# Reordering five seams of a two-block language-model kernel: opening, output operand, first up pairs, start of the down product, gate end

## The reference

```python
# block 1
u = rmsnorm(h, norm_mix); proj = u @ w_in
h = h + concat([sliding_window_sink_attention(q, k, v), gated_deltanet(...)]) @ w_o
m = rmsnorm(h, norm_mlp); h = h + square(relu(m @ w_up)) @ w_down
gate = sigmoid(rmsnorm(h, norm_ple) @ w_ple_gate); h = h + gate * (p @ w_ple_proj)
x = rmsnorm(h, norm_final)
# block 2
u = rms_norm(x, norm_mix_g) @ w_in_2
x = x + concat([pool_mixer(u_pool), hgrn2_mixer(...)]) @ w_out_2
h2 = rms_norm(x, norm_mlp_g_2); x = x + square(relu(h2 @ w_up_2)) @ w_down_2
out = rms_norm(x, final_norm_g_2)
```

## Time and profile before

| | us |
|---|---|
| median of 3 runs | 2700.65 (2698.46 to 2703.38) |
| the profiled execution, its own time | 2696.92 |
| its span, first to last instruction | 2695.1 |
| PE busy in the span | 2551.9 (95%) |
| DVE / POOL / ACT busy | 1953.6 / 1077.8 / 956.4 |

### The profile page before, as it was taken

One profiled execution on the slowest core, in us unless ns is written; L12 is line 12 of the kernel. 1 busy time (PEld: TensorE's weight loads), 2 busy tenths in 40 slices (PEclk: granted clock), 3 DMA queues, 4 the chain that ended last, 5 costly groups with the idle time before them and its releaser, 6 DMA issues. The chain is left out here.

```text
span 2695.1 us, 34099 instructions
## 1 busy us (share of the span) xinstructions
PE 2551.9 (95%) x12634; PEld 2073.5 (77%) x12634; DVE 1953.6 (72%) x2511; ACT 956.4 (35%) x1452; POOL 1077.8 (40%) x675
## 2 busy tenths in 40 slices
PE   8889999989999998999998999999899999999997
PEld 5757887878678887887777788888786888778885
DVE  3677565564878789888948666767558787798887
ACT  3154232131633334444423133333316333344343
POOL 3412112142345555445444433333333555454443
PEclk9999999999999999999999999999999999999999
DMA  4200000021044346444111200000211443554342
GB/s 156 71 16 23 15 18 23 16 86 32 24 158 151 139 161 219 172 169 159 47 48 47 104 32 31 31 26 29 94 40 63 146 159 137 208 195 140 126 156 94
DMA packets 109375, 253.53 MB, mean 94 GB/s; under 512 B 9280, under 2 KB 9536, under 8 KB 107072
## 3 DMA queue, kind: packets, MB, share of 16 engines
q1 hardware_dynamic: 104112, 234.15, 24.9%
q10 hardware_dynamic: 5136, 17.70, 2.0%
HBM read 182.08 MB, written 67.11 MB: 92 GB/s over the span
## 5 line engine op out<-in xcount | busy, mean ns | idle before, releaser
L607 PE MATMUL pairs<-x_hi,w_hi 128*128 128x512 f32 x1592 | 554.2, 412 | 55.8 <-DVE x_lo L1476 15.3
L607 PE MATMUL pairs<-x_lo,w_hi 128*128 128x512 f32 x1592 | 530.6, 397 | 0.0
L607 PE MATMUL pairs<-x_hi,w_lo 128*128 128x512 f32 x1592 | 528.9, 396 | 0.0
L571 POOL TENSOR_TENSOR idle<-idle 128x1 f32<-128x1 f32 x78 | 26.7, 342 | 936.8 <-PE pairs L607 924.0
L607 PEld LDWEIGHTS pairs<-x_hi,w_hi 128*128 128x128 f32 x1592 | 289.3, 192 | 139.6 <-issue 66.8
L607 PEld LDWEIGHTS pairs<-x_hi,w_lo 128*128 128x128 f32 x1592 | 301.1, 191 | 63.9
L607 PEld LDWEIGHTS pairs<-x_lo,w_hi 128*128 128x128 f32 x1592 | 301.3, 191 | 63.4
L607 PE MATMUL mid<-work_r,w_hi 128*128 128x512 f32 x992 | 315.2, 400 | 26.0 <-POOL w_lo L590 12.3
L607 PE MATMUL pairs<-work_r,w_hi 128*128 128x512 f32 x1072 | 329.9, 391 | 4.1 <-DVE work_r L1476 1.8
L590 POOL TENSOR_TENSOR w_lo<-w_raw,w_hi 128x512 fp32r<-128x512 f32 x150 | 237.3, 1589 | 236.5 <-ACT w_hi L1074 236.4
L590 POOL TENSOR_TENSOR w_lo<-work,w_hi 128x512 fp32r<-128x512 f32 x128 | 178.5, 1396 | 221.5 <-ACT w_hi L1074 221.4
(11 more groups left out here) (192 smaller groups left out, 4250.6 us busy)
## 6 DMA issues: line engine op xcount, KB each, us to landing
h_ops<-work SPq DMA_DIRECT2D x224, 256.0 KB, 4.3
w_raw<-w_stream SPq DMA_DIRECT2D x81, 512.0 KB, 3.5
w_raw<-w_up SPq DMA_DIRECT2D x120, 256.0 KB, 3.9
out_sq<-h_ops SPq DMA_DIRECT2D x28, 1024.0 KB, 5.0
x_lo_raw<-h_ops SPq DMA_DIRECT2D x28, 1024.0 KB, 5.0
work<-w_down SPq DMA_DIRECT2D x16, 1024.0 KB, 7.1
out_sq<-w_down SPq DMA_DIRECT2D x8, 1024.0 KB, 7.2
x_lo_raw<-w_down SPq DMA_DIRECT2D x8, 1024.0 KB, 5.4
```

Of the source, the lines that this page charges most:

```text
L571: nc.gpsimd.tensor_tensor(idle[:, 0:1], idle[:, 1:2], idle[:, 1:2], ALU.add)
L607: return nc.tensor.matmul(out, w, x, start=start, stop=stop)
```

## The change

1. **Opening.** Unit 1 is loaded ahead of tile 2, the constants behind tile 6. ACT makes `x_hi` and the square of a tile one after the other. PE runs unit 1 four parts behind unit 0, in alternation; the sums of squares come in two groups of four, after the last part of unit 0 with its partner and after the next part of unit 1; `log_rows` comes before the last part of unit 1. `unit_started` of unit 1 is raised at its fifth part.
2. **`proj_with_norm`** (first unit of each MLP): squares in two groups of four, after the parts of tiles 1 and 3 (before: six groups after the parts of tiles 0 to 5), `log_rows` after the part of tile 5 (before: after all).
3. **Output operand.** The last but one head of both mixers is taken out of the hardware loops of ACT and DVE (`then_last`). In it `mix` tiles 0 to 5 are split: in the delta rule tiles 0 and 1 around the head's norm on ACT and DVE and 2 to 5 after it, in HGRN2 all six after it, and before the head's last `take`. The last head splits tile 6 alone.
4. **First up pairs.** `up_sum(1, 3)` moves from the first up step to right after `up_sum(1, 2)`, ahead of the plain pair's results (`first_y`).
5. **Start of down.** SP loads A11 of the first chunk between two groups of stores of pair 14, and the second operand (`load_h(1)`) after A12. The half slots of the first eight down steps are taken in the order in which the up steps leave them (`slot_index`, `slot_user`), so ACT prepares steps 105 to 110 four ahead (before: 106 and 107 from step 104 on); it makes none at 107 and 110 and two at 108 and 111.
6. **Gate end.** `x_hi` and `x_lo` of tiles 1 to 7 go in one row ahead of the last two tiles' squares and adds.

```diff
+        def slot_index(g):
+            if g < U_STEPS:
+                return (1, 0, 2, 3)[g % 4]
+            turn, k = divmod(g - U_STEPS, 4)
+            return ((0, 2, 3, 1), (0, 2, 1, 3), (0, 1, 2, 3))[min(turn, 2)][k]
+        def slot_user(g):
+            return max(k for k in range(g) if slot_index(k) == slot_index(g))
...
             for j in range(KT):
                 sp.dma_start(res[:, j, :], x_t[:, j, :]).then_inc(x_in[j], 16)
                 if j == 1:
+                    sp.dma_start(w_raw[:, 1, :], w_stream[1]).then_inc(w_loaded[1], 16)
+                if j == 6:
                     sp.dma_start(cst[:, :], consts).then_inc(consts_in, 16)
-                if j == 3:
-                    sp.dma_start(w_raw[:, 1, :], w_stream[1]).then_inc(w_loaded[1], 16)
...
                         load_h(0)
-                        load_h(1)
-                        store_rest(i - 1)
-                    store_last(i - 1)
...
+                        store_rest(i - 1, (2, 7))
                         sp.wait_ge(s["step_done"], g + 3)
                         load_down(0, A11)
+                        store_rest(i - 1, (5, 6))
+                        store_last(i - 1)
                         load_down(0, A12)
+                        load_h(1)
...
-                    for j in ((0, 1), (2,), (3,), (4,), (5,), (6, 7), (), ())[kt]:
-                        square_sum(n, j, squares[j])
-                log_rows(n)
+                    if kt in (1, 3):
+                        for j in range(2 * kt - 2, 2 * kt + 2):
+                            square_sum(n, j, squares[j])
+                    elif kt == KT - 3:
+                        log_rows(n)
...
-            att_unit(0)
-            pe.wait_ge(consts_in, 16)
-            proj_with_norm(1, 1, 0, [mix[:, j, :] for j in range(KT)])
+            LAG = 4
+            for kt in range(KT + LAG):
+                if kt < KT:
+                    part_of_product(0, 0, 0, 0, [kt], KT, 0, P, X_HI, X_LO, x_count=1)
+                if kt == LAG:
+                    pe.wait_ge(w_split, 2)
+                if kt >= LAG:
+                    part_of_product(1, 1, 1, 1, [kt - LAG], KT, 0, P, X_HI, X_LO, enter=KT - LAG)
+                if kt in (KT - 1, KT):
+                    if kt == KT - 1:
+                        pe.wait_ge(consts_in, 16)
+                    for j in range(4 * (kt - KT + 1), 4 * (kt - KT + 2)):
+                        square_sum(0, j, mix[:, j, :])
+                elif kt == KT + 2:
+                    log_rows(0)
...
                 gain_hi(G_MIX, j)
-            for j in range(KT):
                 a(mix[:, j, :], res[:, j, :], ACT.Square, sq_done)
...
+            def mix_hi(v_out, tiles_):
+                act.wait_ge(pair_full, v_out)
+                for j in tiles_:
+                    a(x_hi[:, j, :], mix[:, j, :], ACT.Copy, hi_done)
...
                 a(tmp[:, 0, :], mid01, ACT.Square, s["o_act"])
+                if then_last:
+                    mix_hi(V_WO, range(2))
...
                 a(tmp[:, 0, :], tmp[:, 0, :], ACT.Exp, s["o_act"], scale=-0.5)
+                if then_last:
+                    mix_hi(V_WO, range(2, KT - 2))
...
-                    elif U_STEPS <= g < U_STEPS + 4:
-                        act.wait_ge(s["step_done"], g0 + U_STEPS - (3, 0, 2, 1)[g - U_STEPS])
                     else:
-                        act.wait_ge(s["step_done"], g0 + g - 3)
+                        act.wait_ge(s["step_done"], g0 + slot_user(g) + 1)
...
-                    for ahead in {U_STEPS - 3: (), U_STEPS - 2: (), U_STEPS - 1: (2, 3), U_STEPS: (3, 4)}.get(g, (4,)):
+                    for ahead in {U_STEPS + 2: (), U_STEPS + 3: (3, 4), U_STEPS + 5: (), U_STEPS + 6: (3, 4)}.get(g, (4,)):
...
-                if m == KT - 1:
-                    gain12_hi([1, 2])
-                if m >= 1:
+                if 1 <= m < KT - 1:
                     two_squares(m - 1)
+            gain12_hi(range(1, KT - 1))
+            act.wait_ge(res_done, KT)
+            gain12_hi([KT - 1])
             nc.scalar.preload_act_table_set("natural_log_exp_and_others")
-            gain12_hi([3])
+            two_squares(KT - 2)
             two_squares(KT - 1)
-            gain12_hi(range(4, KT))
...
                     dve.wait_ge(s["o_step"], bump(h, 2, 3))
+                if then_last:
+                    split_mix(1, range(2, KT - 2))
                 take_next(3)
...
                     if k == 0:
                         if i > 1:
                             h_sums(i - 1)
-                        up_sum(i, 3)
+                            up_sum(i, 3)
...
                 up_sum(1, 2)
+                up_sum(1, 3)
                 dve.wait_ge(r_ready, factor_ready(norm))
...
-                if m >= 1:
+                if 1 <= m < KT - 1:
                     two_adds(m - 1)
-            gain12_lo([3])
+            gain12_lo(range(2, KT))
+            two_adds(KT - 2)
             two_adds(KT - 1)
-            gain12_lo(range(4, KT))
```

More of the change, by code:

```diff
@@ L459, in store, with store_rest @@
                     sp.dma_start(h_ops[p - 1, :, i, :], OP_OUT[p]).then_inc(h_stored[p], 16)
[L461 to L469, removed]
+                def store_rest(i, which=(2, 7, 5, 6)):
+                    for p in which:
+                        if p == 2:
+                            sp.wait_ge(s["up_h"], (b * NPAIR + i) * 4 + 4)
+                        else:
+                            sp.wait_ge(s["up_t"], (b * NPAIR + i) * 4 + (7, 5, 6).index(p) + 1)
+                        store(i, p)
                 def store_last(i):
@@ L1161, in _ @@
                     exps(i + 2)
+            def mix_hi(v_out, tiles_):
+                act.wait_ge(pair_full, v_out)
+                for j in tiles_:
+                    a(x_hi[:, j, :], mix[:, j, :], ACT.Copy, hi_done)
             def split_mix(n, v_out, done, count, src):
-                act.wait_ge(pair_full, v_out)
                 act.wait_ge(s[done], count)
-                for j in range(KT - 1):
-                    a(x_hi[:, j, :], mix[:, j, :], ACT.Copy, hi_done)
+                mix_hi(v_out, [KT - 2])
                 for j in range(KT - 1):
@@ L1421, in _, with hg_head @@
                   scale=par[:, P_SCALE + j:P_SCALE + j + 1])
-            def hg_head(h, last=False):
+            def hg_head(h, last=False, then_last=False):
                 if last:
@@ L1461, in hg_head @@
                 a(tmp[:, 0, :], tmp[:, 0, :], ACT.Exp, s["ho_act"], scale=-0.5)
-            with act.Fori(0, HG_H - 1) as h:
+                if then_last:
+                    mix_hi(V_WO2, range(KT - 2))
+            with act.Fori(0, HG_H - 2) as h:
                 hg_head(h)
+            hg_head(HG_H - 2, then_last=True)
             hg_head(HG_H - 1, last=True)
@@ L1630, in dn_head @@
                 if not nxt:
-                    split_mix(1, range(KT - 1))
+                    split_mix(1, [KT - 2])
                 def take_next(k):
@@ L1735, in dn_head @@
                     conv(h, 0, ahead=1)
+                if then_last:
+                    split_mix(1, range(2))
                 dve.wait_ge(s["o_act"], bump(h, 3, 3))
@@ L2115, in hg_head @@
                 if not nxt:
-                    split_mix(5, range(KT - 1))
+                    split_mix(5, [KT - 2])
                 def level_arg(n):
@@ L2204, in hg_head @@
                     dve.wait_ge(s["hg_o_step"], bump(h, 2, 3))
+                if then_last:
+                    split_mix(5, range(KT - 2))
                 take_next(3)
-            with dve.Fori(0, HG_H - 1) as h:
+            with dve.Fori(0, HG_H - 2) as h:
                 hg_head(h, True)
+            hg_head(HG_H - 2, True, then_last=True)
             hg_head(HG_H - 1, False)
```

26 lines of the change are left out of this document (13 added, 13 removed).

## The result

The changed kernel took 2678.66 us in the median of 4 runs (2675.92 to 2681.9), the kernel before 2702.02 beside it (4 runs, 2698.46 to 2706.64): a ratio of 0.992, 95% interval 0.9902 to 0.9938, so 23.4 us gained (16.8 to 26.5). In a later session the same two gave 0.9914 (0.99 to 0.9928). The forecast was 2669.8, range 2658 to 2686; its sum was 30.9, and about three quarters of that came.

The account below looks back on a forecast made before the run. PE, busy 95%, was taken as the bound, with time recoverable only where it waits or runs at half clock. 6.3 + 0 + 2.1 + 11.7 + 8.8 + 2.0 = 30.9 us took 2700.65 to 2669.8; range 2658 to 2686.

Parts of the forecast that it names:

- waits only move: At each seam a shorter wait takes the old one's place, half clock stays: 15 us gained, 2685.5; chance 0.24.
- More comes back: After shorter waits at the seams the clock never falls and `down_sums` catches up: 41 us, 2660; chance 0.13.
- Slower: Heads outside the loops are new code for ACT and DVE: from 15 us each, 2702 or more; chance 0.02.

## Why the prediction was right, and where its sizes were off

The direction and the range held, and so did the mechanism in the main: waits shrink, and at the opening and the pairs a half clock window goes with each. The forecast's own range, 2663 to 2678, was missed by 0.7 us. Part of the closeness is luck: four terms were too large and three too small. Term by term, with the table:

1. **Opening**, 6.3 forecast, 5.7 measured. Unit 2 began at 41.2 for 40.0, its wait was 0.90 for "about 1.1", and the half clock behind it went (0.72 in the earlier trace rows, 1.00 after; none there in any of the seven profiles with the edit). The missing 1.2 us come from the wait of 1.91 at 17.26. POOL had unit 1's weights split in time, at 16.1, as the forecast wanted; but it was its splitting that made a tile of x late:

```profile
13.73 2.39 POOL L583 TENSOR_TENSOR w_lo<-w_raw,w_hi 128x1024 fp32r<-128x1024 f32 x1
14.11 5.49 DVE L1513 SCALAR_TENSOR_TENSOR x_lo<-res,par,x_hi 128x1024 fp32r<-128x1024 f32 x3 [0.71 <-ACT x_hi L1099]
```

The first of these three subtractions, tile 3's, took 3.09 us in place of 1.28, and PE's fourth part began at 17.26, where the forecast had four parts done by 17.5. In the other six kernels with this opening it took 2.6 to 3.1.
2. **`proj_with_norm`**, 0 forecast, about 1.6 measured, by profiles alone: the stage of steps 0 to 9 is 0.3 us shorter in each MLP with it than in the kernels with the pairs alone (30.2 and 30.5), and the 53.6 us ahead of the second MLP's first step (53.6 to 53.7 in eight profiles) are 53.2 in the six with it; in the first MLP 68.1 became 67.6.
3. **Output operand**, 2.1 forecast, about 4.4 measured: 3.0 in the delta rule, 1.4 in HGRN2 (the 4.0 of the table also hold part 2 and the half clock near 670). This is the reading that failed. PE's first part came 5.6 us sooner, as said, but its eighth 2.9 sooner and not 1 (both counted from the ones squares). In the kernel before, the sixth part began at 556.18, when the sixth `x_lo` ended, so PE's end there was set by DVE's row and not by the half clock. DVE after:

```profile
534.35 2.35 DVE L1509 TENSOR_TENSOR x_lo<-work,x_hi 128x1024 fp32r<-128x1024 f32 x2
...
539.19 6.82 DVE L1509 TENSOR_TENSOR x_lo<-work,x_hi 128x1024 fp32r<-128x1024 f32 x4
...
547.06 1.21 DVE L1509 TENSOR_TENSOR x_lo<-work,x_hi 128x1024 fp32r<-128x1024 f32 x1
```

The last subtraction ended 19.3 us behind the start of the ones squares before (557.26 and 537.92) and 16.6 after (548.27 and 531.65), 2.7 sooner for a forecast of 1.1: DVE's idle times ahead of the norm and in it closed, as said, and one long subtraction fewer stands in the row (2.06 and 3.41 us among seven before, 3.40 alone after, 1.2 the others). The half clock had hardly a part in it: without the edit 62.1 us passed with 6.8 us of half clock and 62.8 in the one profile with 10.2; two of the six profiles of the changed kernel and its variants still have 3.4 us behind the first wait, four have none, and all six took 59.2. In HGRN2 the wait went from 4.98 to 3.50, and 6.8 us of half clock stayed in five of the six. The rule of the Trainium skill in "SBUF — State Buffer", section "Who interferes with whom", from which the prediction worked out that this part would give nothing, was right on its cause (POOL's `w_lo` of 3.09 us met the four subtractions that took 6.82) and the outcome drawn from it was not. The heads taken out of the loops, which the forecast weighed only as a loss, gave 1.2.
4. **First up pairs**, 11.7 forecast, 9.7 at the seams together with part 2. Steps 8 and 9 still lost 1.6 where I left 0.8 (the forecast's own 754.0 and 753.5 give 0.5): the wait is for POOL's piece, 1.37. What failed is the unwritten 0 for the steps behind it: 1.2 and 1.6 us came back by step 104, as the mean of groups whose ranges overlap. That PE without its lag meets the chain of load, sums, copy and piece is my reading of the single steps of 2.8 to 3.4 us. The 3.9 us that the first two profiles show in the second MLP are 1.6 of this and 2.3 of chance, as the profile of before has the shortest such stage of fourteen (257.24).
5. **Start of down**, 8.8 forecast, 4.6 measured, and 0.9 given back later. This is the step that was most mis-sized. Step by step, both MLPs together, means of the profiles of that row: step 104 took 3.8 us less, steps 105 and 106 took 3.3 more, steps 113 to 116 took 4.1 less. The forecast took the loss at step 105 for one of weights, with the fourth operand tile 2.3 us late behind it. It was 3.5 us of wait for the third and fourth tile and 3.4 of half clock; and step 105 had been at 6.4 in the mean before, with waits of 0.22 and 1.36 for the same two tiles behind that of 2.76 for the weights, so that little was left to win there. DVE's instructions of 0.69 us took 1.28 and 1.78 beside POOL's pieces, four of them in this place where the kernel before has two (1.34 and 1.76). The forecast had used just that row for the output operand and not here. Putting the splits sooner took 3.7 us off with such meetings still there (1.77 and 1.76), so how much is the meetings' and how much the order's isn't shown.
6. **Gate end**, 2.0 forecast, 0.4 measured, 0.0 by the run of it alone. The wait of some 4 us ahead of the `sum_rows` and the half clock in them were forecast (3.91; 1.7). Not forecast: the half clock fell on the very matmuls whose end starts the chain that PE meets 44 us later, so that it counted in full, at 2.8, and the half clock behind the earlier wait (3.4 us from 1453.8) was still there.

The time lies between the forecast and the rival *waits only move*, 8.9 us above the one and 6.8 below the other. That rival was right on the first up pairs (6 by it; 9.7 less the 2.8 given back), on the start of down (4; 4.6 less 0.9) and on the gate end (0; 0.4), and in each DVE or POOL took the old place, as it said. It was wrong on the opening (4.6; 5.7), where the half clock went, and on the output operand (0.5; 4.4). *More comes back* had nothing for it: DVE did not catch up at steps 105 to 116. *Slower* had a slip of its own: 15 us for each head on top of the forecast is 2700, not 2702.

The rule of the Trainium skill in "TensorE: Matmul & The Clock Gate", section "What's actually happening", that activity lifts the clock from a default of half rate, fits the gate end (a wait of 3.91 us, then 6.41 for 3.59 us of work) and the pairs, where a wait of 1.37 left the clock at 1.00.

## What to carry to other kernels

When a transfer or a weight piece is brought forward, look at what its consumers' engines do at the new time: at the opening the piece itself was on time and made the operand beside it late (3.09 us for 1.28). Before a stall is priced by its last wait, ask what each engine would have waited for next: step 105 was late for its weights and, right behind, for its operand. Price the steps behind a removed stall too, not the stall alone: of 9.7 us won at the pairs 2.8 came back. And put filler work ahead of a wait whose successor starts a long chain: three parts moved ahead of two sums, with no work added, took their stage from 205.4 us (four profiles) to 203.7 (three).

## What the runs showed that I had not expected

- Taking one pass out of the hardware loops of ACT and DVE shortened three heads by 1.2 us (305.5 to 304.3; ranges 0.1 and 0.3 wide) in the delta rule, and by nothing in HGRN2.
- Half clock of 6.8 to 10.2 us near 670 in nine of fourteen profiles and none in five, with the same instructions there: two profiles of one kernel differ by 3.5 us in one stage by that alone (67.6 and 71.1 from the matmul that stood at 659.91 before to the first step).
- A SCALAR_TENSOR_TENSOR of 128x512 with both inputs in SBUF took 1.28 us beside POOL's subtraction and 0.69 otherwise, as the plain TENSOR_TENSOR did (1.78 and 0.68).
